# One of two lower parts of each u block subtracted by VectorE in place of TensorE

## The chip, the cores and the metric

The kernel runs on one core of one Trainium2 chip. The metric is the device time of one execution in microseconds (us), the median of the runs. A profiled execution gives, beside the time, the order of the instructions on each engine. Engines are named as in the profile: PE is TensorE (PEld its weight loads), DVE is VectorE, ACT is ScalarE, POOL is GpSimd, SP is SyncE, which here only starts DMAs.

## The reference

One step of an encoder layer for 1024 prompt tokens and 64 sample tokens: gated attention, convolution and memory branches, and then a retrieval of single-neuron experts (PEER). The change touches only the expert part, which computes, for tokens `xb` in blocks of 128:

```python
q = (xb @ w_q).reshape(B, PEER_HEADS, 2, PEER_DK // 2)
s1 = jnp.einsum('bhd,hkd->bhk', q[:, :, 0], keys1).astype(jnp.float32)
s2 = jnp.einsum('bhd,hkd->bhk', q[:, :, 1], keys2).astype(jnp.float32)
v1, i1 = lax.top_k(s1, PEER_TOPK)
v2, i2 = lax.top_k(s2, PEER_TOPK)
...
top, pos = lax.top_k(cand, PEER_TOPK)
idx = jnp.take_along_axis(cidx, pos, axis=-1)
g = jax.nn.softmax(top, axis=-1).astype(xb.dtype)
ue = u[idx]
ve = v[idx]
act = jax.nn.gelu(jnp.einsum('bd,bhkd->bhk', xb, ue), approximate=False)
return jnp.einsum('bhk,bhkd->bd', g * act, ve)
```

`u` and `v` are tables of 16384 rows of 1024 float32 numbers. Each token and each of 8 heads picks 16 rows of each.

## The kernel before

The front (projections), the attention and an opening stage for the first tile of tokens come first, up to about 1300 us. Then the function `experts` runs nine tiles of up to 128 tokens in steps, one step for one picked row per token. For the early tiles the step gathers a row of `u` for each token (GpSimd's indirect DMA, `u_row`), VectorE multiplies it with the token's normed row and sums (`dot`, line 3272), ScalarE applies gelu to four dots at a time (`gelu`, line 3088), and VectorE adds the gathered row of `v` times its weight (`vector_sum`, line 3295), eleven steps after the dot.

For the last four tiles (512 tokens, `TABLED`) no rows of `u` are gathered. TensorE computes instead the products of all 16384 rows of `u` with the 512 tokens, while the early tiles' steps go on. This is the table stage, steps 150 to 390 (`TABLE_STEPS`). The table of `u` is read in 128 blocks of 128 rows (`load_block`, a ring of three blocks). The products run in the reduced format fp32r, so each operand is split into an upper part (rounded to fp32r) and a lower part (what is left), and each product of two operands is three: upper by upper, upper by lower, lower by upper. For one block b:

- `turn_block` (line 2799): TensorE transposes the block's eight 128x128 squares into the PSUM tile `pH` (`open_h_T_ps`), four squares in each of two halves. A half is one PSUM bank of 128x512.
- `upper` (line 3017): ScalarE copies the half out of PSUM rounded to fp32r, into `B.uh`.
- `less_upper` (line 2805): TensorE adds to the same bank the product of minus identity with `B.uh`, so that the bank holds the lower part.
- `lower` (line 3021): ScalarE copies the bank into `B.ul`.
- `products` (line 2821): 8 x 3 products of 128x128 by 128x512 into the bank b % 2 of `pQS`.
- `stage_scores` (line 3028): ScalarE copies these scores to a buffer, which SyncE stores every fourth block.

The engines run their own lists of instructions in order. The lists are written by loops over the same step number n, and `units_at` spreads 257 table units over the 240 steps, for TensorE and for ScalarE alike: one unit opens the table, then each block has two. TensorE's unit 2b+1 holds `products(b, 0..3)` and the turn of half 0 of block b+1, its unit 2b+2 holds `products(b, 4..5)`, `less_upper` of half 0, the turn of half 1, `products(b, 6..7)` and `less_upper` of half 1. In 17 steps there are two units. In ScalarE's step n gelu comes before the table unit, exponentials of the routing (`exps`, line 2986) after it.

VectorE's step n holds the dot, the sum, and then the pieces of the routing (the two top-k, one hot rows and indices of the next heads, `route`), and three steps after a head's last piece its `gate` (line 3222), which waits for ScalarE's exponentials. VectorE has one piece of table work: `lower_h` (line 3323), the lower part of the 512 tokens' rows, at step 151.

After the table the scores are stored to memory and loaded again in another order (`load_scores`, line 2607), and picked from: TensorE, `pick_rows` (line 2878), VectorE, `picked` (line 3336), from step 398 on. The last tiles then sum rows of `v` on VectorE and on TensorE (`row_sum`, line 2904).

Of the kernel before, what the change touches and what calls it, by code (L numbers as in the profile page):

```python
# [13 lines left out]
F32 = mybir.dt.float32  # L14
# [7 lines left out]
P = 128  # L22
# [23 lines left out]
S0 = 1  # L46
# [2377 lines left out]
def experts(nc, io, scr, c, L, p, banks, done):  # L2424
# [29 lines left out]
    s_sck, s_const, s_pconst, s_hh, s_hl = (after() for _ in range(5))  # L2454
    s_uturn, s_uh, s_less, s_ul, s_block, s_stage = (after() for _ in range(6))
    s_keys, s_spread, s_skept, s_hot, s_pick, s_fpick, s_fold, s_tgelu, s_twt = (after() for _ in range(9))
    x_p = io["x_prompt"][0].rearrange("(t p) d -> t p d", p=P)[1:]
# [252 lines left out]
    def tensor(pe):  # L2710
# [81 lines left out]
        def turn_block(b, half):  # L2792
            pe.wait_ge(s_uin[b % TABLE_RING].sem, s_uin[b % TABLE_RING].start + 16 * (b // TABLE_RING + 1))
            if b:
                pe.wait_ge(s_ul.sem, s_ul.start + TURNS * (b - 1) + half + 1)
            else:
                pe.wait_ge(s_hT, S0 + NE + 1)
            for k in range(4):
                ins = pe.matmul(pH[:, half, k * P:(k + 1) * P], B.u[b % TABLE_RING][:, (4 * half + k) * P:(4 * half + k + 1) * P], c.ident[:],  # L2799
                                is_transpose=True, start=(k == 0), stop=False, skip_group_check=True)  # L2800
            ins.then_inc(s_uturn.sem, 1)

        def less_upper(b, half):
            pe.wait_ge(s_uh.sem, s_uh.start + TURNS * b + half + 1)
            pe.matmul(pH[:, half, :], B.minus[:], B.uh[b % 2][:, 4 * half:4 * half + 4, :].rearrange("p k i -> p (k i)"),  # L2805
                      start=False, stop=True, skip_group_check=True).then_inc(s_less.sem, 1)

        def products(b, ks):
            if ks[0] % 4 == 0:
                pe.wait_ge(s_ul.sem, s_ul.start + TURNS * b + ks[0] // 4 + 1)  # L2810
            if ks[0] == 0:
                if b >= 2:
# [12 lines left out]
        def table():  # L2825

            pe.wait_ge(s_const.sem, s_const.start + 1)
            for half in range(TURNS):
                turn_block(0, half)
                less_upper(0, half)  # L2830
            yield
            for b in range(NK):
# [5 lines left out]
                if b + 1 < NK:  # L2838
                    less_upper(b + 1, 0)
                    turn_block(b + 1, 1)  # L2840
                products(b, range(6, 8))
                if b + 1 < NK:
                    less_upper(b + 1, 1)
                yield

        def turn_keys(t):
            i = t - FIRST_TABLED
            pe.wait_ge(s_keys.sem, s_keys.start + NH * (i + 1))
            if i == 0:
                pe.wait_ge(s_const.sem, s_const.start + 2)  # L2850
                pe.wait_ge(s_ul.sem, s_ul.start + TURNS * NK)
            pe.wait_ge(s_skept.sem, s_skept.start + SPREADS * i)
# [79 lines left out]
    def scalar(act):  # L2932
# [85 lines left out]

        def lower(b, half):
            act.wait_ge(s_less.sem, s_less.start + TURNS * b + half + 1)  # L3020
            act.activation(B.ul[b % 2][:, 4 * half:4 * half + 4, :], pH[:, half, :].rearrange("p (k i) -> p k i", i=P), ACT.Copy).then_inc(s_ul.sem, 1)  # L3021

# [7 lines left out]
        def table():  # L3030
# [6 lines left out]
            act.activation(B.hh[:], B.h[:], ACT.Copy).then_inc(s_hh.sem, 1)  # L3037
            for half in range(TURNS):
                upper(0, half)
                lower(0, half)  # L3040
            yield
            for b in range(NK):
                if b + 1 < NK:
                    upper(b + 1, 0)
                yield
                if b + 1 < NK:
                    lower(b + 1, 0)
                    upper(b + 1, 1)
                    lower(b + 1, 1)
                stage_scores(b)  # L3050
                yield
# [69 lines left out]
    def vector(dve):  # L3121
# [198 lines left out]
        def lower_h():  # L3320

            dve.wait_ge(s_hh.sem, s_hh.start + 1)
            dve.tensor_tensor(B.hl[:], B.h[:], B.hh[:].bitcast(F32), ALU.subtract).then_inc(s_hl.sem, 1)

        def picked(t, g):
            i = PICKS * (t - FIRST_TABLED) + g
# [21 lines left out]
        tail = done.vector(dve, ahead)  # L3348
        front_units = front()
        for n in range(AHEAD_ROWS, STEPS + VECTOR_LAG):  # L3350
# [12 lines left out]
            for _ in units_at(FRONT_UNITS, FRONT_STEPS, n - 2):  # L3363
                next(front_units)
            if n == TABLE_STEPS[0] + 1:
                lower_h()
            for R, piece in ROUTES_AT.get(n, ()):
# [115 lines left out]
```

## Time and profile before

| | us |
|---|---|
| median of three runs | 3690.84 |
| lowest, highest | 3690.61, 3699.87 |
| span of the profiled execution | 3696.7 |
| its own time | 3699.87 |

The span goes from the first to the last instruction. The profiled execution's own time is the highest of the three, the only one that is not below the span; 3.2 us lie around the span. Busy times count an engine's instructions without waits. An idle time is put down to what released the engine at its end. Over the whole span the granted clock of TensorE is 0.950 in the mean.

### The profile page before, as it was taken

How to read it: one execution, taken by the hardware profiler on the slowest of the kernel's cores; microseconds unless marked ns; L12 is line 12 of the kernel's file. 1: busy time of each engine (PE TensorE's matmuls, PEld its weight loads, DVE VectorE, ACT ScalarE, POOL GpSimd, SP SyncE). 2: the span in 40 equal slices, each digit the busy share in tenths (PEclk: the TensorE clock that was granted, in tenths of full speed). 3: DMA queues.
4: the chain of work that ended last, by engine and by line, in shares of the span. 5: the costliest groups of instructions: out<-in, count | busy, mean ns of one | idle time of the engine just before them, and what ended most of it. 6: DMA issues, size and time to landing. Idle time of an engine off the chain costs nothing. (4 is left out here: it accounts for less than half of the span.)

```text
span 3696.7 us, 44443 instructions
## 1 busy us (share of the span) xinstructions
PE 3314.5 (90%) x13218; PEld 2187.7 (59%) x13218; DVE 2943.3 (80%) x6713; ACT 1413.4 (38%) x2912; POOL 2212.0 (60%) x1831
## 2 busy tenths in 40 slices
PE   8999899899999979988799999999968799988765
PEld 7787555544444446666688887888834355555321
DVE  5499764367887968999988898988889698987655
ACT  5235675222442322332444454445434333333200
POOL 6221144055565646777766675766656676777876
PEclk9999999999999989998899999999978899999989
DMA  6415564698999999999999999999999999999999
GB/s 213 127 40 147 137 179 174 207 359 315 350 376 384 340 382 349 375 383 374 408 400 403 379 405 406 388 401 388 395 403 357 361 373 391 390 387 360 333 366 344
DMA packets 443310, 1224.36 MB, mean 331 GB/s; under 512 B 65250, under 2 KB 153478, under 8 KB 442047
## 3 DMA queue, kind: packets, MB, share of 16 engines
q0 software_dynamic: 239616, 872.52, 61.7%
q1 hardware_dynamic: 177162, 313.45, 24.4%
q10 hardware_dynamic: 26293, 35.54, 2.8%
q8 instruction: 108, 1.77, 0.2%
q14 instruction: 131, 1.07, 0.1%
HBM read 1129.03 MB, written 92.31 MB: 330 GB/s over the span
## 5 line engine op out<-in xcount | busy, mean ns | idle before, releaser
L2679 POOL DMA_INDIRECT late_v_rows<-in_peer_v,late_kept_idx x573 | 605.3, 1056 | 195.2 <-issue 168.9
L2666 POOL DMA_INDIRECT late_u_rows<-in_peer_u,late_kept_idx x320 | 490.9, 1534 | 267.3 <-DVE late_dots L3272 187.9
L3272 DVE CUSTOM_DVE_ANT_0 late_u_rows<-late_u_rows,open_rows_ps 128x1024 f32<-128x1024 f32 x432 | 522.3, 1209 | 11.2 <-DMA late_u_rows<-in_peer_u,late_expert_idx 10.8
L3295 DVE SCALAR_TENSOR_TENSOR late_x<-late_v_rows,late_weights,late_x 128x1024 f32<-128x1024 f32 x368 | 471.2, 1280 | 0.0
L2821 PE MATMUL open_q_and_scores_ps<-table_h_T_upper,table_u_T_upper 128*128 128x512 f32 x1024 | 424.4, 415 | 0.0
L2821 PE MATMUL open_q_and_scores_ps<-table_h_T_lower,table_u_T_upper 128*128 128x512 f32 x1024 | 402.5, 393 | 0.0
L2821 PE MATMUL open_q_and_scores_ps<-table_h_T_upper,table_u_T_lower 128*128 128x512 f32 x1024 | 401.6, 392 | 0.0
L2679 POOL DMA_INDIRECT late_u_rows<-in_peer_v,late_kept_idx x259 | 293.8, 1134 | 93.5 <-issue 78.5
L1841 POOL DMA_INDIRECT open_u_rows<-in_peer_u,late_expert_idx x115 | 166.0, 1443 | 255.1 <-DVE late_dots L2281 125.9
L3295 DVE SCALAR_TENSOR_TENSOR late_x<-late_v_rows,table_weights,late_x 128x1024 f32<-128x1024 f32 x155 | 198.5, 1280 | 73.9 <-DMA late_v_rows<-in_peer_v,late_kept_idx 63.8
L2904 PE MATMUL open_sums_ps<-late_v_rows,table_diag 128*128 128x512 f32 (+1 forms) x328 | 184.1, 696 | 68.6 <-DMA late_v_rows<-in_peer_v,late_kept_idx 42.4
L3017 ACT ACTIVATE table_u_T_upper<-open_h_T_ps 128x512 fp32r<-128x512 f32 x256 | 152.4, 595 | 232.1 <-PE open_h_T_ps L2799 201.4
L3021 ACT ACTIVATE table_u_T_lower<-open_h_T_ps 128x512 fp32r<-128x512 f32 x256 | 152.9, 597 | 228.6 <-PE open_h_T_ps L2805 189.7
L3295 DVE SCALAR_TENSOR_TENSOR late_x<-late_u_rows,table_weights,late_x 128x1024 f32<-128x1024 f32 x138 | 176.9, 1282 | 65.7 <-DMA late_u_rows<-in_peer_v,late_kept_idx 59.5
L3065 ACT ACTIVATE table_apart<-open_h_T_ps,table_less_lane 128x512 bf16<-128x512 f32 x128 | 87.6, 684 | 362.1 <-PE open_h_T_ps L2862 241.9
L2821 PEld LDWEIGHTS open_q_and_scores_ps<-table_h_T_upper,table_u_T_lower 128*128 128x128 f32 x1024 | 192.9, 188 | 44.4
L2821 PEld LDWEIGHTS open_q_and_scores_ps<-table_h_T_lower,table_u_T_upper 128*128 128x128 f32 x1024 | 194.2, 190 | 32.6
L2821 PEld LDWEIGHTS open_q_and_scores_ps<-table_h_T_upper,table_u_T_upper 128*128 128x128 f32 x1024 | 193.9, 189 | 31.7
L497 POOL TENSOR_TENSOR front_w_lower<-front_w_raw,front_w_upper 128x512 fp32r<-128x512 f32 x62 | 94.7, 1546 | 193.5 <-ACT front_w_upper L721 192.4
L1177 POOL TENSOR_SCALAR attn_probs<-attn_probs,attn_row_scale 128x256 f32<-128x256 f32 (+2 forms) x68 | 93.1, 1374 | 171.7 <-DVE attn_row_scale L1290 171.7
L3336 DVE SCALAR_TENSOR_TENSOR table_masked<-table_row,table_first_keys,open_q_and_scores_ps 128x128 f32<-128x128 f32 x512 | 146.6, 342 | 51.7 <-DMA scr_mqT<-front_turned 28.1
L896 DVE SCALAR_TENSOR_TENSOR front_x_and_conv_y<-front_conv_input_T,front_conv_taps,front_x_and_conv_y 128x1118 f32<-128x1118 f32 x120 | 176.9, 1474 | 2.0
(471 smaller groups left out, 7803.0 us busy)
## 6 DMA issues: line engine op xcount, KB each, us to landing
table_u_block<-in_peer_u SPq DMA_DIRECT2D x128, 512.0 KB
scr_scores<-table_scores SPq DMA_DIRECT2D x32, 1024.0 KB
open_weight_columns<-in_w_in SPq DMA_DIRECT2D x64, 256.0 KB
table_first_scores<-scr_scores SPq DMA_DIRECT2D x4, 4096.0 KB
table_second_scores<-scr_scores SPq DMA_DIRECT2D x4, 4096.0 KB
front_w_raw<-in_w_in SPq DMA_DIRECT2D x48, 256.0 KB, 5.9
scr_m<-open_gated SPq DMA_DIRECT2D x42, 256.0 KB
late_v_rows<-in_peer_v,late_kept_idx POOLq DMA_INDIRECT x573
```

The costliest lines, as they stand in the source:

```text
L497: pool.tensor_tensor(wl[b][:, k, :], raw[:, k, :], wh[b][:, k, :].bitcast(F32), ALU.subtract).then_inc(s_wl, 1)
L896: ins = dve.scalar_tensor_tensor(yj, a[:, k:k + CONV_OUT], taps[:, j, k:k + 1], yj, ALU.mult, ALU.add)
L1841: pool.indirect_dma_start(O.u[b][:], None, io["peer_u"][0], bass.IndirectOffsetOnAxis(ap=rows_of(n), axis=0)).then_inc(s_u[b], 16)
L2666: pool.indirect_dma_start(u[k % U_RING][:], None, io["peer_u"][0], bass.IndirectOffsetOnAxis(ap=rows_of(n), axis=0)).then_inc(s_u[k % U_RI ...
L2679: pool.indirect_dma_start(slot[:], None, io["peer_v"][0], bass.IndirectOffsetOnAxis(ap=rows_of(m), axis=0)).then_inc(arrived, 16)
L2821: ins = pe.matmul(pQS[:, b % 2, 0:TABLE_COLS], us[b % 2][:, k, :], hs[:, k, :], start=(k == 0 and i == 0), stop=(k == KC - 1 and i == 2))
L2904: ins = pe.matmul(banks_of(t)[0:rows, h, :], diag[k % DIAGS][:, 0:rows], slot[:, h * BANK:(h + 1) * BANK], start=(m == first_of(t)), stop= ...
L3017: act.activation(B.uh[b % 2][:, 4 * half:4 * half + 4, :], pH[:, half, :].rearrange("p (k i) -> p k i", i=P), ACT.Copy).then_inc(s_uh.sem, 1)
L3021: act.activation(B.ul[b % 2][:, 4 * half:4 * half + 4, :], pH[:, half, :].rearrange("p (k i) -> p k i", i=P), ACT.Copy).then_inc(s_ul.sem, 1)
L3272: dve.tensor_tensor_reduce(u[k % U_RING][:], u[k % U_RING][:], h2_rows, 1.0, 0.0, ALU.mult, ALU.add, dots[:, n % COLS:n % COLS + 1]).then_ ...
L3295: dve.scalar_tensor_tensor(rows[:], slot[:], weight_of(m), rows[:], ALU.mult, ALU.add).then_inc(s_vsum, 1)
L3336: ins = dve.scalar_tensor_tensor(B.masked[:, q, :], B.row[:], B.first_keys[:, at:at + 1], pQS[:, i % 2, q * P:(q + 1) * P], ALU.is_equal, ...
```

## The change

The second half of each block (squares 4 to 7) is split in another way. TensorE turns it into its bank, ScalarE copies the upper part, and then VectorE reads the turned rows from PSUM, subtracts the upper part and writes the lower part to `B.ul` (`lower_half`), in one instruction of 128x512. TensorE's product with minus identity and ScalarE's second copy are left out for this half. The first half stays as it was. VectorE gets a list of table units on the same steps as the other engines: the unit that opens the table holds `lower_h` (one step earlier than before) and `lower_half(0)`, and the second unit of block b holds `lower_half(b + 1)`. It stands after the dot and the sum of its step and before the routing pieces. A new semaphore, `s_vl`, counts VectorE's halves; TensorE waits for it before `products(b, 4..)` and before it turns the next block's second half.

```diff
+    s_vl = p.sem("second_lower_halves")
...
         def turn_block(b, half):
             pe.wait_ge(s_uin[b % TABLE_RING].sem, s_uin[b % TABLE_RING].start + 16 * (b // TABLE_RING + 1))
-            if b:
-                pe.wait_ge(s_ul.sem, s_ul.start + TURNS * (b - 1) + half + 1)
+            if b and half:
+                pe.wait_ge(s_vl, S0 + b)
+            elif b:
+                pe.wait_ge(s_ul.sem, s_ul.start + b)
...
-        def less_upper(b, half):
-            pe.wait_ge(s_uh.sem, s_uh.start + TURNS * b + half + 1)
-            pe.matmul(pH[:, half, :], B.minus[:], B.uh[b % 2][:, 4 * half:4 * half + 4, :].rearrange("p k i -> p (k i)"),
+        def less_upper(b):
+            pe.wait_ge(s_uh.sem, s_uh.start + TURNS * b + 1)
+            pe.matmul(pH[:, 0, :], B.minus[:], B.uh[b % 2][:, 0:4, :].rearrange("p k i -> p (k i)"),
                       start=False, stop=True, skip_group_check=True).then_inc(s_less.sem, 1)
...
         def products(b, ks):
-            if ks[0] % 4 == 0:
-                pe.wait_ge(s_ul.sem, s_ul.start + TURNS * b + ks[0] // 4 + 1)
+            if ks[0] == 0:
+                pe.wait_ge(s_ul.sem, s_ul.start + b + 1)
+            elif ks[0] == 4:
+                pe.wait_ge(s_vl, S0 + b + 1)
...
@@ def table(): (TensorE)
                 products(b, range(4, 6))
                 if b + 1 < NK:
-                    less_upper(b + 1, 0)
+                    less_upper(b + 1)
                     turn_block(b + 1, 1)
                 products(b, range(6, 8))
-                if b + 1 < NK:
-                    less_upper(b + 1, 1)
...
@@ def table(): (ScalarE)
                 if b + 1 < NK:
-                    lower(b + 1, 0)
+                    lower(b + 1)
                     upper(b + 1, 1)
-                    lower(b + 1, 1)
                 stage_scores(b)
...
+        def lower_half(b):
+            dve.wait_ge(s_uh.sem, s_uh.start + TURNS * b + 2)
+            if b >= 2:
+                dve.wait_ge(s_block.sem, s_block.start + b - 1)
+            dve.tensor_tensor(B.ul[b % 2][:, 4:8, :], pH[:, 1, :].rearrange("p (k i) -> p k i", i=P), B.uh[b % 2][:, 4:8, :].bitcast(F32), ALU.subtract).then_inc(s_vl, 1)
+
+        def table():
+
+            lower_h()
+            lower_half(0)
+            yield
+            for b in range(NK):
+                yield
+                if b + 1 < NK:
+                    lower_half(b + 1)
+                yield
...
-            if n == TABLE_STEPS[0] + 1:
-                lower_h()
+            for _ in units_at(TABLE_UNITS, TABLE_STEPS, n):
+                next(table_units)
```

## Rows read from the trace of the kernel before

**Rows 1.** The page, part 1: busy us (share of the span) and instructions by engine.

```profile
PE 3314.5 (90%) x13218; PEld 2187.7 (59%) x13218; DVE 2943.3 (80%) x6713; ACT 1413.4 (38%) x2912; POOL 2212.0 (60%) x1831
```

**Rows 2.** Busy by stretch: us; PE, PEld, DVE, ACT, POOL; clock; DMA share; GB/s.

```profile
1784.00:2694.00 910.00, 890.33 (x4352) 727.54 (x4352) 794.63 (x1798) 443.38 (x810) 605.74 (x487) 0.99 1.02 397
2260.00:2300.00 40.00, 35.68 (x165) 28.87 (x164) 36.09 (x87) 16.27 (x30) 27.56 (x24) 0.91 1.03 411
```

**Rows 3.** Waits, 1784 to 2694 us: waiter, releaser, us in all, times, longest.

```profile
ACT table_u_T_upper L3017 <- PE open_h_T_ps L2799: 201.4, 111, 6.9
...
POOL late_u_rows L2666 <- DVE late_dots L3272: 172.5, 106, 11.3
DVE late_exp_scale L3222 <- ACT late_exps L2986: 104.0, 23, 9.9
...
PE open_h_T_ps L2805 <- ACT table_u_T_upper L3017: 12.9, 9, 7.7
...
DVE late_exp_scale L3222 <- issue: 1.3, 1, 1.3
```

**Rows 4.** Instruction groups, same stretch: count, busy us, mean ns, idle before.

```profile
L3295 DVE SCALAR_TENSOR_TENSOR late_x<-late_v_rows,late_weights,late_x 128x1024 f32<-128x1024 f32 x242 | 309.9, 1281 | 0.0
L3272 DVE CUSTOM_DVE_ANT_0 late_u_rows<-late_u_rows,open_rows_ps 128x1024 f32<-128x1024 f32 x242 | 292.5, 1209 | 0.4
...
L3021 ACT ACTIVATE table_u_T_lower<-open_h_T_ps 128x512 fp32r<-128x512 f32 x256 | 152.9, 597 | 228.6 <-PE open_h_T_ps L2805 189.7 <-issue 35.9 <-DVE late_side_idx L3150 2.0
```

**Rows 5.** Score evictions (ns, first and last start); one block in order of time.

```profile
L3028 ACT ACTIVATE table_scores<-open_q_and_scores_ps x128: 589/592/598, 1805.4 to 2693.9; 128x512 f32<-128x512 f32 x128
...
2203.56 0.59 ACT L3028 ACTIVATE table_scores<-open_q_and_scores_ps 128x512 f32<-128x512 f32 x1
...
2207.46 0.40 PE L2805 MATMUL open_h_T_ps<-table_u_T_upper,table_minus_identity 128*128 128x512 f32 x1
2207.69 0.60 PE L2799 MATMUL open_h_T_ps<-identity,table_u_block 128*128 128x128 f32 x4
...
2210.45 0.59 ACT L3028 ACTIVATE table_scores<-open_q_and_scores_ps 128x512 f32<-128x512 f32 x1
```

**Rows 6.** Front subtraction (group); two neighbours in VectorE's queue, order of time.

```profile
L834 DVE TENSOR_TENSOR front_turned_lower<-front_turned_ps,front_turned 128x512 f32<-128x512 f32 x6 | 4.1, 683 | 0.0
...
2282.20 0.69 DVE L3181 TENSOR_TENSOR late_one_hot<-late_pos_split_f,late_iota 128x512 f32<-128x512 f32 x1
2282.81 1.22 DVE L3272 CUSTOM_DVE_ANT_0 late_u_rows<-late_u_rows,open_rows_ps 128x1024 f32<-128x1024 f32 x1
```

**Rows 7.** Order of time at the start of the table stage.

```profile
1782.75 1.28 DVE L3295 SCALAR_TENSOR_TENSOR late_x<-late_v_rows,late_weights,late_x 128x1024 f32<-128x1024 f32 x1
...
1784.55 3.60 ACT L3037 ACTIVATE table_h_T_upper<-table_h_T 128x4096 fp32r<-128x4096 f32 x1
...
1788.18 4.43 DVE L3323 TENSOR_TENSOR table_h_T_lower<-table_h_T,table_h_T_upper 128x4096 fp32r<-128x4096 f32 x1 [0.77 <-ACT table_h_T_upper L3037]
...
1795.03 0.60 ACT L3017 ACTIVATE table_u_T_upper<-open_h_T_ps 128x512 fp32r<-128x512 f32 x1 [0.25 <-PE open_h_T_ps L2799]
```

**Rows 8.** VectorE, order of time: step 388, first picks, a late row.

```profile
2680.32 1.20 DVE L3272 CUSTOM_DVE_ANT_0 late_u_rows<-late_u_rows,open_rows_ps 128x1024 f32<-128x1024 f32 x1
...
2726.36 0.35 DVE L3336 SCALAR_TENSOR_TENSOR table_masked<-table_row,table_first_keys,open_q_and_scores_ps 128x128 f32<-128x128 f32 x1 [7.97 <-PE open_q_and_scores_ps L2878]
...
2740.55 1.28 DVE L3295 SCALAR_TENSOR_TENSOR late_tile_sum<-late_v_rows,late_weights,late_tile_sum 128x1024 f32<-128x1024 f32 x1 [5.34 <-issue]
```

**Rows 9.** ScalarE, order of time: a table load and its gelu.

```profile
1599.86 1.28 ACT L3088 ACT_TABLE_LOAD   x1
1604.93 0.20 ACT L3088 ACTIVATE late_gelu<-late_dots 128x4 f32<-128x4 f32 x1 [3.79 <-DVE late_dots L3272]
```

**Rows 10.** Order of time around 2270 and 2280 us.

```profile
2269.88 0.51 PE L2805 MATMUL open_h_T_ps<-table_u_T_upper,table_minus_identity 128*128 128x512 f32 x1 [0.24 <-ACT table_u_T_upper L3017]
...
2280.43 0.60 ACT L3017 ACTIVATE table_u_T_upper<-open_h_T_ps 128x512 fp32r<-128x512 f32 x1 [6.86 <-PE open_h_T_ps L2799]
```

More of the change, by code:

```diff
@@ L2799, in turn_block @@
                 ins = pe.matmul(pH[:, half, k * P:(k + 1) * P], B.u[b % TABLE_RING][:, (4 * half + k) * P:(4 * half + k + 1) * P], c.ident[:],
-                                is_transpose=True, start=(k == 0), stop=False, skip_group_check=True)
+                                is_transpose=True, start=(k == 0), stop=(half == 1 and k == 3), skip_group_check=True)
             ins.then_inc(s_uturn.sem, 1)
-        def less_upper(b, half):
-            pe.wait_ge(s_uh.sem, s_uh.start + TURNS * b + half + 1)
-            pe.matmul(pH[:, half, :], B.minus[:], B.uh[b % 2][:, 4 * half:4 * half + 4, :].rearrange("p k i -> p (k i)"),
+        def less_upper(b):
+            pe.wait_ge(s_uh.sem, s_uh.start + TURNS * b + 1)
+            pe.matmul(pH[:, 0, :], B.minus[:], B.uh[b % 2][:, 0:4, :].rearrange("p k i -> p (k i)"),
                       start=False, stop=True, skip_group_check=True).then_inc(s_less.sem, 1)
         def products(b, ks):
-            if ks[0] % 4 == 0:
-                pe.wait_ge(s_ul.sem, s_ul.start + TURNS * b + ks[0] // 4 + 1)
+            if ks[0] == 0:
+                pe.wait_ge(s_ul.sem, s_ul.start + b + 1)
+            elif ks[0] == 4:
+                pe.wait_ge(s_vl, S0 + b + 1)
             if ks[0] == 0:
@@ L2827, in table @@
             pe.wait_ge(s_const.sem, s_const.start + 1)
-            for half in range(TURNS):
-                turn_block(0, half)
-                less_upper(0, half)
+            turn_block(0, 0)
+            less_upper(0)
+            turn_block(0, 1)
             yield
@@ L2850, in turn_keys @@
                 pe.wait_ge(s_const.sem, s_const.start + 2)
-                pe.wait_ge(s_ul.sem, s_ul.start + TURNS * NK)
+                pe.wait_ge(s_ul.sem, s_ul.start + NK)
+                pe.wait_ge(s_vl, S0 + NK)
             pe.wait_ge(s_skept.sem, s_skept.start + SPREADS * i)
@@ L3017, in upper, with lower @@
             act.activation(B.uh[b % 2][:, 4 * half:4 * half + 4, :], pH[:, half, :].rearrange("p (k i) -> p k i", i=P), ACT.Copy).then_inc(s_uh.sem, 1)
-        def lower(b, half):
-            act.wait_ge(s_less.sem, s_less.start + TURNS * b + half + 1)
-            act.activation(B.ul[b % 2][:, 4 * half:4 * half + 4, :], pH[:, half, :].rearrange("p (k i) -> p k i", i=P), ACT.Copy).then_inc(s_ul.sem, 1)
+        def lower(b):
+            act.wait_ge(s_less.sem, s_less.start + b + 1)
+            act.activation(B.ul[b % 2][:, 0:4, :], pH[:, 0, :].rearrange("p (k i) -> p k i", i=P), ACT.Copy).then_inc(s_ul.sem, 1)
         def stage_scores(b):
@@ L3037, in table @@
             act.activation(B.hh[:], B.h[:], ACT.Copy).then_inc(s_hh.sem, 1)
-            for half in range(TURNS):
-                upper(0, half)
-                lower(0, half)
+            upper(0, 0)
+            lower(0)
+            upper(0, 1)
             yield
@@ L3348, in vector @@
         tail = done.vector(dve, ahead)
-        front_units = front()
+        front_units, table_units = front(), table()
         for n in range(AHEAD_ROWS, STEPS + VECTOR_LAG):
```

## The prediction

> **What bounds the kernel now.** I first read the table of engines for the whole span [rows 1]: no engine is at its limit everywhere, so the stage that the change touches is read by itself. The busy time by stretch over the table stage (1784 to 2694 us) shows TensorE busy for 890.3 of 910 us, VectorE for 794.6, ScalarE for 443.4, at a granted clock of 0.99 [rows 2]. The waits of the same stretch say who waits for whom [rows 3]: TensorE's longest row of waits is 12.9 us, while VectorE waits 104.0 us in 23 pieces for `late_exps` of ScalarE. ScalarE does those exponentials behind its table work, and the table work waits for TensorE (201.4 us before `upper`, 189.7 before `lower`, [rows 3, 4]). So VectorE runs ahead, is held at each head's gate, and TensorE sets the pace. GpSimd waits for VectorE's dots (172.5 us), and neither dots nor sums show VectorE waiting for a gathered row (0.4 and 0.0 us) [rows 4]: the gathers are not what ends last here, though DMA moves 397 GB/s.
>
> TensorE's pace is in the order of time [rows 5]: the 128 score evictions start from 1805.4 to 2693.9 us, 7.00 us apart in the mean, and two undisturbed neighbours are 2210.45 - 2203.56 = 6.89 us apart. The product with minus identity holds TensorE for 0.23 us, from its start to the next (2207.46 to 2207.69), and I take the same for each of the 24 products of that width.
>
> **What goes.** One 128x512 product per block leaves TensorE: 128 x 0.23 = 29.4 us, all on the path as long as TensorE sets the pace. Its block becomes 6.89 - 0.23 = 6.66 us. One eviction of 0.597 us per block leaves ScalarE (128 x 0.597 = 76 us, [rows 4]): ScalarE is busy less than half the stage, so this is worth nothing by itself; it only lets the remaining evictions and exponentials start sooner.
>
> **What comes.** 128 subtractions of 128x512 on VectorE, one input in PSUM, output in fp32r. The table stage has none, but the front does the same subtraction (turned PSUM tile less its upper part): 683 ns [rows 6]. In a full queue the next instruction starts sooner: a 0.69 us operation at 2282.20 is followed by one at 2282.81 [rows 6], so one costs 0.61 us net; bounds 0.61 and 0.69. I take 0.61, since VectorE's queue is full there: 128 x 0.61 = 78.1 us (88 at the upper bound). A rule that speaks against the change: the Trainium skill, "VectorE: DVE Perf Modes", section "The DRAIN you can't avoid", says that the next operation doesn't start until the pipe of the last has emptied. If that charged the whole 0.683 us the sum would come out 9 us later; the starts 0.61 us apart in the row contradict it here, so the row is used.
>
> **Who bounds after it.** VectorE waits 104.0 + 1.3 + 0.77 = 106.1 us of the stage [rows 3, 7]; these waits exist because it is ahead, and they go when it isn't. Work of VectorE outside those waits: 910 - 106.1 = 803.9 us, plus 78.1 = 882. TensorE by itself: 128 x 6.66 = 852 plus its stalls. So VectorE becomes the bound, and it is tied to TensorE block by block: `lower_half(b+1)` waits for ScalarE's upper copy, which waits for TensorE's turn in the same step, while TensorE's products 4 to 7 wait for `lower_half`. Behind the waiting subtraction stand VectorE's routing pieces, the next dot and the next sum; for the dots wait GpSimd's gathers and ScalarE's gelu.
>
> **The start.** In the old order VectorE subtracts `h_T` at step 151 with 0.77 us of wait. Now its first unit stands in step 150: its sum there ends at 1784.03, the upper copy of h at 1788.15, so it waits 4.1 us; the subtraction ends at 1792.6 [rows 7]. The second upper copy of block 0 ends at 1795.6 [rows 7], so `lower_half(0)` waits another 3.1 us. 7.2 us of waits come (the old 0.77 is in the 106.1).
>
> **The end of the stage.** Before, VectorE reaches its first picked rows with 7.97 us of idle time before 2726.36, so its last work ended at 2718.4 [rows 8]. That wait is for a chain from the last product (2693.9) through the score eviction, store and load to the first pick: 32.4 us. New arrival of VectorE: 2718.4 - 106.1 + 7.2 + 78.1 = 2697.6. New end of the chain: the dot of step 388 was at 2680.32 [rows 8]; it comes at 2680.3 - 106.1 + 7.2 + 77.5 = 2658.9; dot, sum and the last `lower_half` take 2.3 + 0.1 + 0.6, twelve products 2.8, then 32.4: 2697.1. The two meet. Against 2726.4 both are 28.8 us early. After that every engine has the same work, and the rings of rows tie them together, so I let the shift pass to the end. One gathered row comes 5.34 us late at 2740.55 [rows 8]; that may move by as much either way.
>
> **What coupling gives back.** (a) Gelu stands in ScalarE's queue every fourth step ahead of the copies, and waits for the dot of that step, which so far was long done. With VectorE last it is not. In about 30 of 60 cases it stands before the copy that `lower_half` waits for: gelu 0.20 and two copies 0.5 + 0.6, with a hand-off, 1.5 us, beside VectorE's sum of 1.28: 0.2 us each, 6 us. The table load is not in it: the one at 1599.86 ran before gelu's 3.79 us wait [rows 9]. (b) 257 units lie in 240 steps, so 17 steps hold two. There two `lower_half` are one step of VectorE's work apart (803.9 / 240 = 3.35 us). From one `lower_half` TensorE needs six products (1.4), `less_upper` (0.23) and a turn (0.60), ScalarE 0.60 and a hand-off, to make the next one possible: 3.0 us, and up to 4.7 where gelu stands between. I take 0.3 us each, 5 us. (c) The u blocks behind the store and load of a tile's sums come late once: `upper` at 2280.43 stands after 6.86 us of idle time [rows 10]. Now VectorE, which had been in front, feels it, less TensorE's lead of some 3 us: 4 us. (d) 127 hand-offs where the queue no longer overlaps fully: 3 us. Sum 18 us; ends 2 us (all hidden) and 41 us (0.3 us per block more than I take: the nearest row is the 0.24 us of idle that TensorE shows between an upper copy's end and its product, 2269.88 [rows 10]).
>
> So -28.8 + 18 = -10.8 us. The profiled execution has a span of 3696.7 us and 3.2 us around it, 3699.87 in all, and would take 3689.1. It lies 9.0 us above the median, 3690.84; taken from that the time is 3680.
>
> **Rivals.**
> *TensorE remains the bound (0.15).* If the subtractions hide in the 106.1 us of waits, 127 x 0.23 = 29 us are won: 3662. For it: 106.1 is more than 78.1. Against it: the waits come from being ahead, and the start and the coupling take 25 us of the rest.
> *The loop closes badly, slower (0.20).* The place is ScalarE's queue: gelu(n) waits for dot(n), the copy for `lower_half(b+1)` waits behind gelu, and VectorE stands at it. Priced at 0.2 us for 30 blocks above; if each costs 1.0 us, and the odd steps (where gelu holds TensorE's `less_upper`) 0.5 us, it is 45 us for 6: -10.8 + 39 = +28, 3719; at 0.6 us each and nothing for the odd steps, 18 for 6, it is +1. It decides from about 0.6 us per coincidence. For it: the lead that kept ScalarE from waiting (VectorE's waits reach 9.9 us, [rows 3]) vanishes. Against it: in a block of two steps VectorE needs 2 x 3.35 + 0.61 = 7.3 us from one `lower_half` to the next, and the copy is there after 3.0 to 4.7.
> *The losses equal the gain (0.10).* No mechanism but the sum of (a) to (d) near 29 us: 3691.
> *TensorE's clock (0.10).* With VectorE as the bound TensorE idles 0.3 us a block. After the long stall the granted clock over 2260 to 2300 was 0.91 against 0.99 in the stage [rows 2], which puts part of it at the lower level, 1.2 GHz. If such spells, worth some 3.5 us each, come ten times, TensorE is late by 35 us; its slack against VectorE is 882 - 852 = 30 us over the whole stage, little of it where a spell falls, and I let it take a third: +23 - 10.8 = +12, 3703. By the Trainium skill's page "TensorE: Matmul & The Clock Gate", Part 1, the throttled rate is the default and activity releases it; by that rule idle time spread thinly costs nothing, and the stage's 0.99 agrees as far as it goes.
> *The change doesn't do what it says:* the products' order and every wait's count follow the removed signals; I see no way for it.
>
> **Numbers.** The forecast's own case has 0.45; its own range is 3670 to 3691. Of it 0.27 lies beyond 0.3% (11 us, about what this measurement can tell from no change) and 0.18 within. Faster: 0.27 + 0.15 = 0.42. Same: 0.18 + 0.10 = 0.28. Slower: 0.20 + 0.10 = 0.30. The range reaches down to the first rival, 3662, and up to 3703, which leaves out the far part of the second.
>
> **What would show it.** `less_upper` x128 instead of 256; VectorE's subtraction near 0.68 us; waits for `late_exps` in the stage below 15 us in place of 104; new idle time of TensorE before products (4..5) until VectorE, of some 0.3 us per block; VectorE busy over 96% of the stage; the last score eviction near 2683 in place of 2693.9, and the first picked rows near 2715. Wrong, if VectorE still waits over 60 us in the stage, at `lower_half` above all, or if TensorE's clock shows new spells at the lower level.

## The result and the profile after

The changed kernel takes 3708.7 us in the median of 20 runs, the kernel before 3698.47 in 20 runs beside it. The ratio is 1.0028, with a 95% interval of 1.0019 to 1.0037: about 10 us slower. A second batch of runs gave 1.0038 (1.0022 to 1.0053). The forecast was 10.8 us faster, 3680 us, with a range up to 3703. (It was counted from 3690.84, the median of three runs; the differences here are from the 20.) The profiled execution took 3722.61 us, 14 above its median, so the argument below goes by stretches of it and not by its end.

The waits of the changed kernel, 1784 to 2720 us (waiter, what released it, us in all, times, longest), answer to [rows 3]:

```profile
ACT table_u_T_upper L3021 <- PE open_h_T_ps L2802: 216.7, 95, 5.3
POOL late_u_rows L2667 <- DVE late_dots L3275: 190.6, 178, 12.7
ACT late_gelu L3091 <- DVE late_dots L3275: 132.8, 52, 8.8
ACT table_u_T_lower L3025 <- PE open_h_T_ps L2808: 80.7, 88, 1.0
...
DVE table_u_T_lower L3332 <- ACT table_u_T_upper L3021: 28.4, 22, 4.0
...
PE open_q_and_scores_ps L2826 <- ACT table_u_T_lower L3025: 22.3, 22, 2.2
...
PE open_h_T_ps L2808 <- ACT table_u_T_upper L3021: 17.7, 15, 7.7
...
PE open_q_and_scores_ps L2826 <- DVE table_u_T_lower L3332: 0.6, 2, 0.3
```

VectorE's 104 us of waits for the exponentials are gone altogether: VectorE no longer runs ahead, as forecast. Three rows are new. VectorE waits 28.4 us for the upper copies. ScalarE's gelus, which had no row in this stretch, wait 132.8 us for VectorE's dots. And TensorE waits 22.3 us at the first product of a block for `lower`, ScalarE's copy of the first half. Its wait at `less_upper` (line 2805 before, 2808 now) grew from 12.9 us to 17.7, of which 7.7 lie at the start in both kernels. For VectorE's half, where some 0.3 us per block had been forecast, it waits 0.6 us in all.

The new subtraction, in the group rows (us busy, mean ns, idle before), and the same stretch from the dot of step 150 to the dot of step 388, first the kernel before, then the changed one, then its second trace. Columns as in [rows 2].

```profile
L3332 DVE TENSOR_TENSOR table_u_T_lower<-open_h_T_ps,table_u_T_upper 128x512 fp32r<-128x512 f32 x128 | 87.8, 686 | 31.6 <-ACT table_u_T_upper L3021 28.4 <-issue 2.1
```

```profile
1781.60:2680.30 898.70, 876.73 (x4291) 716.94 (x4292) 783.46 (x1772) 439.12 (x801) 596.83 (x480) 0.99 1.02 397
```

```profile
1784.70:2691.90 907.20, 859.84 (x4196) 696.73 (x4197) 862.25 (x1897) 378.60 (x682) 613.00 (x480) 0.99 1.02 395
```

```profile
1785.50:2693.40 907.90, 861.92 (x4196) 698.73 (x4197) 862.41 (x1899) 378.39 (x682) 613.12 (x480) 0.98 1.02 394
```

The stretch is 8.5 us longer (907.2 against 898.7), and the second trace repeats it within 0.7 us. VectorE's busy time rose by 862.25 - 783.46 = 78.8 us, to 95.0% of the stretch; TensorE's is nearly the same (859.84 us), so the two engines set the pace between them. From the dot of step 388 to that of step 447 the two kernels take the same, 202.1 us before and 201.7 after. So the loss up to step 447 lies in the table stage, and it is about as large as the loss of the whole. Behind step 447 the time differs from one batch to the next whatever the kernel (the changed kernel took 827 us in the first trace and 787 in the second), and nothing is argued from it.

Adding up VectorE's idle times in that stretch by their length gives this account (worked out from the trace's single instructions):

| VectorE, steps 150 to 388, us | before | changed |
|---|---|---|
| busy | 783.5 | 862.2 |
| waits over 0.5 us | 106.1 | 32.2 |
| shorter gaps | 9.2 | 12.7 |
| sum | 898.7 | 907.2 |

Of the 32.2 us, 7.2 lie at the start, 4.0 at the late u block at step 279, and 21.0 in fourteen waits at the subtraction, of which twelve (17.6 us; at steps 178, 193, 206, 221, 249, 262, 292, 305, ...) stand within one step of a step that holds two table units. The other two (3.4 us, at steps 195 and 223) stand behind table loads of ScalarE, which are shown further down.

### The profile page after: what moved, and what is told of

Read it like the earlier page. It is cut to its first block and busy times, and to the rows that moved or that the text cites. A ratio compares the mean times of both kernels' runs of the same rounds, so it can differ in the third digit from the quotient of the medians.

```text
span 3720.8 us, 44315 instructions
## 1 busy us (share of the span) xinstructions
PE 3288.5 (88%) x13090; PEld 2162.4 (58%) x13090; DVE 3021.8 (81%) x6841; ACT 1348.2 (36%) x2784; POOL 2239.0 (60%) x1831
## 5 line engine op out<-in xcount | busy, mean ns | idle before, releaser
L2667 POOL DMA_INDIRECT late_u_rows<-in_peer_u,late_kept_idx x320 | 509.1, 1591 | 261.1 <-DVE late_dots L3275 209.3
L2826 PE MATMUL open_q_and_scores_ps<-table_h_T_upper,table_u_T_upper 128*128 128x512 f32 x1024 | 426.7, 417 | 23.0 <-ACT table_u_T_lower L3025 22.3
L2680 POOL DMA_INDIRECT late_u_rows<-in_peer_v,late_kept_idx x259 | 301.7, 1165 | 94.1 <-issue 73.4
L2908 PE MATMUL open_sums_ps<-late_u_rows,table_diag 128*128 128x512 f32 x248 | 133.7, 678 | 51.0 <-DMA late_u_rows<-in_peer_v,late_kept_idx 47.8
```

Source lines behind the costliest of these rows:

```text
L2667: pool.indirect_dma_start(u[k % U_RING][:], None, io["peer_u"][0], bass.IndirectOffsetOnAxis(ap=rows_of(n), axis=0)).then_inc(s_u[k % U_RI ...
L2680: pool.indirect_dma_start(slot[:], None, io["peer_v"][0], bass.IndirectOffsetOnAxis(ap=rows_of(m), axis=0)).then_inc(arrived, 16)
L2908: ins = pe.matmul(banks_of(t)[0:rows, h, :], diag[k % DIAGS][:, 0:rows], slot[:, h * BANK:(h + 1) * BANK], start=(m == first_of(t)), stop= ...
```

## Experiments

The stage figures below are VectorE's times from the dot of step 150 to that of step 388, as above.

### The load without the waits

```diff
 (on the kernel before)
+        def unread(b):
+            ...
+            dve.wait_ge(s_un, S0 + b)
+            dve.tensor_tensor(tile_sum[:, 0:BANK], pRows[:, 1, :], keysT[:, 0:4, :].rearrange("p s k -> p (s k)"), ALU.subtract).then_inc(s_un, 1)
...
+            for _ in units_at(TABLE_UNITS, TABLE_STEPS, n):
+                next(table_units)
```

> The kernel before, with VectorE's 128 subtractions of 128x512 added at the places of the change, but into a tile that nobody reads and with no other engine waiting; TensorE and ScalarE keep all their work. Theory A (the load of 78 us fits into VectorE's 106 us of waits, what hurts is the order in which the three engines now wait for each other): the time of before within 0.15% (ratio 0.999 to 1.002), TensorE's pace still 6.87 us a block, VectorE's waits for the exponentials down from 104 to some 20 to 35 us. Rival B (the load alone does it, VectorE is full and GpSimd's gathers and the rest come late): 8 us or more slower, ratio 1.002 to 1.004, as the changed kernel.

Ratio 1.0010 (0.9999 to 1.0022), 3701.72 us against 3698.67. The stage took 896.6 us, 2.1 less than before. VectorE's waits in the stage:

```profile
DVE late_exp_scale L3223 <- ACT late_exps L2987: 25.8, 14, 5.1
DVE late_exp_scale L3223 <- issue: 1.9, 1, 1.9
```

```profile
1779.20:2675.80 896.60, 877.00 (x4299) 717.80 (x4300) 859.58 (x1897) 440.67 (x804) 616.35 (x480) 0.99 1.02 399
```

VectorE is as busy as in the changed kernel (859.6 us) and the stage isn't longer. The waits for the exponentials fell from 104.0 to 25.8, by the 78 us added. As long as TensorE keeps its old work and sets the pace, the load alone does nothing to the stage; Theory A holds there. The whole time's interval doesn't exclude a loss of up to 8 us, so that part is only bounded.

### The waits without the load

```diff
 (on the changed kernel)
-            dve.tensor_tensor(B.ul[b % 2][:, 4:8, :], pH[:, 1, :]...
+            if b < 2:
+                dve.tensor_tensor(B.ul[b % 2][:, 4:8, :], pH[:, 1, :]...
+            else:
+                dve.tensor_tensor(B.ul[b % 2][:, 4, 0:4], pH[:, 1, 0:4], B.uh[b % 2][:, 4, 0:4].bitcast(F32), ALU.subtract).then_inc(s_vl, 1)
```

> The changed kernel, but from block 2 on VectorE subtracts 4 columns in place of 512, so that all waits stay and most of the load goes (the lower parts of the second halves are then not computed). Theory A (waits between the engines): about 0.5 us per block go from VectorE, 60 us of 78; as VectorE's work was the bound together with the waits, the stage falls to TensorE's pace of about 6.65 us per block or a little above: 20 to 27 us faster than before, ratio 0.9930 to 0.9950, if the waits by themselves cost little without the load; if it stays within 5 us of before the waits alone hold it. Rival B (load): the full 25 to 29 us of TensorE's saving appear, 0.9925 or less.

Ratio 0.9979 (0.9962 to 0.9995); the stage took 880.9 us, 26.3 less than the changed kernel's and 17.8 less than before, with 62 us less for VectorE to do. Both expectations (0.9950 or less) were too good. But neither the load alone nor the waits alone makes the stage longer than before: it takes the two together, at this place in the step. Waits for rows of `v` came up that the changed kernel doesn't have:

```profile
DVE table_u_T_lower L3335 <- ACT table_u_T_upper L3021: 37.1, 22, 6.0
DVE late_x L3298 <- DMA late_v_rows<-in_peer_v,late_kept_idx: 9.5, 14, 2.2
DVE late_x L3298 <- issue: 8.4, 10, 1.8
```

At this pace the gathered rows of `v` come late, 18 us in 24 waits. This comes back in the last experiments.

### The subtraction one unit later

```diff
             lower_half(0)
             for b in range(NK):
+                if b:
+                    lower_half(b)
                 yield
-                if b + 1 < NK:
-                    lower_half(b + 1)
                 yield
```

> The changed kernel with each block's subtraction one table unit later in VectorE's list, that is, one step. Nothing is added or left out. Theory A: VectorE's 25 us of waits at the subtraction (14 of them at the steps with two units) fall below 8 us, since TensorE and ScalarE have a step more to deliver, and the stage shortens by 15 to 20 us against the changed kernel: ratio to before 0.9970 to 0.9995. Rival C (TensorE then waits as long for VectorE as VectorE did for ScalarE, since the half that it needs comes a step later): no better than the changed kernel, 1.002 to 1.004.

Ratio 0.9969 (0.9954 to 0.9985), stage 884.7 us: 22.5 us less than the changed kernel with the very same instructions. VectorE's waits over 0.5 us are 13.1 in place of 32.2, and TensorE's wait for VectorE's half, the price that Rival C named, is 14.3 us in 25 waits, where TensorE has slack. Rival C falls, and the gain is a little above Theory A's range (15 to 20 us, 0.9970). Of the waits at the subtraction 9.2 us are left, where under 8 were expected. The rows, up to 2700 us, which is behind the stage (the waits of 8.8 and 15.4 us lie there):

```profile
ACT late_gelu L3091 <- DVE late_dots L3275: 30.2, 20, 8.8
PE open_sums_ps L2908 <- ACT table_diag L3086: 15.4, 1, 15.4
PE open_q_and_scores_ps L2826 <- DVE table_u_T_lower L3332: 14.3, 25, 1.6
...
DVE table_u_T_lower L3332 <- ACT table_u_T_upper L3021: 9.2, 7, 3.1
```

### Every second block

On the changed kernel, with `by_dve(b)` for `b % 2 == 1`; the other blocks' second halves keep `less_upper` and ScalarE's `lower`.

```diff
-            if b and half:
-                pe.wait_ge(s_vl, S0 + b)
+            if b and half and by_dve(b - 1):
+                pe.wait_ge(s_vl, S0 + dve_halves(b))
...
                 products(b, range(6, 8))
+                if b + 1 < NK and not by_dve(b + 1):
+                    less_upper(b + 1, 1)
```

> The changed kernel, but only every second block's second half is subtracted by VectorE; the others keep TensorE's product and ScalarE's copy. VectorE gets 39 us in place of 78, TensorE is spared 15 us in place of 29. Theory A: VectorE has some 40 us left over, so its waits cost nothing and TensorE remains the bound: 8 to 14 us faster than before, ratio 0.996 to 0.998. Rival C (each wait of the new kind costs by itself): half of the changed kernel's loss, ratio 1.0005 to 1.0015.

Ratio 0.9984 (0.9969 to 0.9998), just outside Theory A's 0.996 to 0.998. The stage took 898.0 us, as before, so Theory A is wrong there: VectorE waits 59.3 us at the subtraction, and the 15 us that TensorE is spared don't show. With slack in VectorE its place in the step still ties the engines.

### The changed kernel again, and gelu behind the unit

Where does a wait at a doubled step come from? ScalarE, TensorE and VectorE of the changed kernel in order of time, around the wait at step 348:

```profile
2540.42 0.20 ACT L3091 ACTIVATE late_gelu<-late_dots 128x4 f32<-128x4 f32 x1 [2.42 <-DVE late_dots L3275]
2540.53 0.58 ACT L3025 ACTIVATE table_u_T_lower<-open_h_T_ps 128x512 fp32r<-128x512 f32 x1
...
2541.16 0.50 PE L2826 MATMUL open_q_and_scores_ps<-table_h_T_upper,table_u_T_upper 128*128 128x512 f32 x1 [0.38 <-ACT table_u_T_lower L3025]
...
2541.63 0.69 DVE L3332 TENSOR_TENSOR table_u_T_lower<-open_h_T_ps,table_u_T_upper 128x512 fp32r<-128x512 f32 x1
...
2546.07 0.60 PE L2802 MATMUL open_h_T_ps<-identity,table_u_block 128*128 128x128 f32 x4
...
2546.77 0.59 ACT L3021 ACTIVATE table_u_T_upper<-open_h_T_ps 128x512 fp32r<-128x512 f32 x1
...
2547.39 0.69 DVE L3332 TENSOR_TENSOR table_u_T_lower<-open_h_T_ps,table_u_T_upper 128x512 fp32r<-128x512 f32 x1 [1.41 <-ACT table_u_T_upper L3021]
```

Gelu waits 2.42 us for VectorE's dot. Behind it in ScalarE's queue stands `lower`, the copy of the first half, and TensorE can't begin the next block's first product without it (2541.16). So when VectorE does its subtraction at 2541.63, TensorE has only begun the twelve products that it could have had behind it. It still has to do those, a turn, six more, `less_upper` and a turn before ScalarE can copy, and VectorE, one step later, waits 1.41 us.

The way is not the same at all twelve doubled steps. Ahead of each, TensorE has waited for a copy that stood behind a waiting gelu: one step before at four of them, for `lower` (0.4 to 2.2 us); two steps before at five, at `less_upper` for the upper copy (0.5 to 1.3 us); three steps before at the last three (178, 206, 262), for `lower` again (0.6 to 1.8 us). What they share is that TensorE comes late to the `less_upper` of the next block: 2.1 to 4.4 us behind the end of VectorE's last subtraction (from the single instructions). From there to the end of the upper copy it is 1.52 us every time.

At steps 195 and 223 ScalarE's queue holds a table load between the exponentials and gelu, ahead of both copies. ScalarE and VectorE around step 223:

```profile
2068.77 1.28 ACT L3091 ACT_TABLE_LOAD   x1
2070.07 0.20 ACT L3091 ACTIVATE late_gelu<-late_dots 128x4 f32<-128x4 f32 x1
2070.18 0.58 ACT L3025 ACTIVATE table_u_T_lower<-open_h_T_ps 128x512 fp32r<-128x512 f32 x1
...
2071.28 0.69 DVE L3332 TENSOR_TENSOR table_u_T_lower<-open_h_T_ps,table_u_T_upper 128x512 fp32r<-128x512 f32 x1 [2.16 <-ACT table_u_T_upper L3021]
```

The next run moves gelu, with its table loads, behind both copies:

```diff
 (ScalarE's step n, on the changed kernel)
-            if n % GROUP == GROUP - 1 and n < STEPS and dotted(n):
+            if n % GROUP == GROUP - 1 and n < STEPS and dotted(n) and not TABLE_STEPS[0] < n < TABLE_STEPS[1]:
                 gelu(n // GROUP)
...
             for _ in units_at(TABLE_UNITS, TABLE_STEPS, n):
                 next(table_units)
+            if n % GROUP == GROUP - 1 and TABLE_STEPS[0] < n < TABLE_STEPS[1]:
+                gelu(n // GROUP)
```

> The changed kernel once more, beside the others of this batch, for a second trace of it. Both theories: ratio to before 1.002 to 1.004; VectorE from the dot of step 150 to that of step 388 in 903 to 911 us (907.2 in the first trace), 12 or more waits of over 0.5 us at the subtraction, nearly all in or next to a step with two table units.

> The changed kernel with ScalarE's gelu of a step placed behind the table unit of that step in place of ahead of it, in the table stage. Theory D (the waits at the steps with two units come from gelu: it waits for VectorE's dot, the lower copy of half 0 queues behind it, TensorE waits for that copy before its first product and so is late when two units fall into one step): VectorE's waits at the subtraction fall from 28 us to 8 to 15, steps 150 to 388 take 886 to 895 us in place of 907, ratio to before 0.9965 to 1.000. Rival E (what is missing at those steps is the time that TensorE and ScalarE need for two units, 3.0 us at the least, against one step of VectorE, gelu or not): the waits stay above 20 us, ratio 1.0015 or more.

The changed kernel again: 1.0038 (1.0022 to 1.0053), stage 907.9 us, sixteen waits at the subtraction, 28.6 us. With gelu behind the unit: 0.9995 (0.9980 to 1.0010), stage 884.5 us, the waits at the subtraction 9.0 us in five. Rival E falls: the time that two units need isn't what was missing. At nine of the same twelve blocks the upper copy now ends 3.06 to 3.25 us behind the last subtraction, where it was 3.6 to 5.9 us before the move. The rows up to 2700 us, again with two waits behind the stage (8.8 and 18.6 us):

```profile
ACT late_gelu L3091 <- DVE late_dots L3277: 28.9, 16, 8.8
PE open_sums_ps L2908 <- ACT table_diag L3086: 18.6, 1, 18.6
PE open_q_and_scores_ps L2826 <- DVE table_u_T_lower L3334: 14.0, 25, 1.3
DVE table_u_T_lower L3334 <- ACT table_u_T_upper L3021: 9.4, 7, 3.7
```

Inside the stage gelu's waits for the dots fall from 119 us in the first trace of the changed kernel (129 in the second) to 15, and TensorE waits for VectorE's half in place of ScalarE's copies, which means that it is nearly always as far ahead as it can be. The run shows that gelu's place is the cause; it doesn't part the ways by which gelu held the others, since gelu stands behind both copies now.

The gain over the changed kernel is 23 us in the stage and some 16 us (1.0038 to 0.9995) in the time. 3.5 us of it are given back between steps 388 and 447 (205.2 us for 201.7); the rest is not explained. Against the kernel before, no gain in the time is shown (the interval holds 1), though the stage is 14 us shorter. One unit later, with as long a stage, has 0.9969, so gelu behind the unit may cost something outside the stage.

### Both together

One unit later and gelu behind the unit.

> Both: the subtraction one unit later and gelu behind the table unit. Theory D: with one unit later nearly all of the waits were gone already (13 us left, 7 of them at the start of the stage), so there is little to add: steps 150 to 388 in 880 to 886 us (884.7 with one unit later alone), ratio within 0.001 of that one's 0.9969. Rival E: the same, since both say that slack is all that counts; a time clearly over it would say that gelu behind the unit does harm elsewhere.

Ratio 0.9983 (0.9969 to 0.9997), stage 886.0 us. Nothing is added, as expected: each edit alone gives the slack. The ratio lies 0.0014 above that of one unit later alone, outside the 0.001 stated, but the two were run in different batches and the intervals overlap.

### Every second block, one unit later

> VectorE subtracts only every second block's second half, and one unit later. Theory A: TensorE is the bound with 15 us saved, VectorE has slack: steps 150 to 388 in 884 to 890 us, 10 to 14 us under before, ratio 0.9965 to 0.9980; no better than one unit later with all blocks, whose bound is VectorE at 885. Rival C (each wait costs by itself, and fewer of them are better): faster than one unit later with all blocks, below 0.9960.

Ratio 0.9961 (0.9947 to 0.9975), stage 882.8 us, 2 us shorter than with all blocks. This version beats both kernels, by 14 us the kernel before. Theory A's ranges (884 to 890 us, 0.9965 or more) were too slow by a little, and Rival C's (below 0.9960) isn't reached. Against one unit later with all blocks (0.9969, another batch) no difference is shown.

### What is late next

Four more on that version: the store of a tile's sums split from the load behind it, the second load of scores later, both, and both with three of four blocks.

```diff
             if b in AFTER_BLOCK:
-                t = AFTER_BLOCK.index(b)
-                store_y(t)
+                store_y(AFTER_BLOCK.index(b))
+            if b - 4 in AFTER_BLOCK:
+                t = AFTER_BLOCK.index(b - 4)
                 load_x2(t + 2)
                 load_h2(t + 2)
```

> Built on the version with every second block and one unit later (every_second_later, ratio 0.9961). Its one edit: the load of the next tile's sums and rows is issued four u blocks after the store that it waits for, so that SyncE's queue doesn't hold back the loads of u blocks for 16 us. Theory: the long block near 2275 us (TensorE 6 to 7 us late, VectorE some 4 us in the changed kernel) goes; steps 150 to 388 take 876 to 879 us in place of 882.8; ratio 0.9940 to 0.9958. Rival (the u blocks' loads are late for want of bandwidth at that place, not for the wait): the stage stays at 881 or more.

Ratio 0.9979 (0.9966 to 0.9993), stage 881.3 us. VectorE's long wait for the late u block at step 280 (7.5 us) is 0.7 us now, so the wait did come from SyncE's queue. But the stage is only 1.5 us shorter, where 4 to 7 were expected; it stays at the 881 or more that the rival named, and the whole time shows no gain. The theory is right about the wait and wrong about its worth. What took its place:

```profile
DVE table_u_T_lower L3355 <- ACT table_u_T_upper L3040: 23.0, 18, 3.4
...
DVE late_x L3321 <- DMA late_v_rows<-in_peer_v,late_kept_idx: 10.1, 16, 1.5
DVE late_x L3321 <- issue: 6.4, 5, 2.0
```

Rows of `v` come late, which in the version before this edit showed no row. The stretch moves 406 GB/s:

```profile
1791.10:2672.40 881.30, 862.24 (x4248) 707.32 (x4249) 824.51 (x1833) 411.80 (x743) 600.26 (x480) 0.99 1.03 406
```

```diff
-        load_scores(FIRST_TABLED)
+        load_scores(FIRST_TABLED, (0,))
         store_y(SHORT - 1)
+        load_scores(FIRST_TABLED, (1,))
...
+                elif k == 0:
+                    sp.wait_ge(s_pick.sem, s_pick.start + 2)
```

> Built on every_second_later. Its one edit: the second of the two loads of 4 MB of scores starts only when two groups have been picked. Theory F (the gathered row of step 401 or so is late since it stands behind 8 MB of scores in the DMA engines): VectorE's waits at the sums between steps 398 and 404 fall from 9.3 us to under 5 us, the dot of step 447 comes 3 to 7 us earlier behind that of 388 than the 204.7 us there. Rival G (a row or a pick is late anyway, since the same bytes have to be moved): the sum of the waits there stays above 13 us of 15.7 and 447 comes 204 us or more behind 388.

Ratio 0.9960 (0.9936 to 0.9985), stage 882.6 us. From step 388 to 447 the time is 202.2 us, 2.5 less than 204.7, and the waits there are 6.4 us at the pick and 6.8 at a row of step 405, 13.2 in place of 15.7. Neither expectation fits whole: the waits at the sums of steps 398 to 404 are gone, as Theory F had it, but less than 3 us are gained and the sum of the waits stays above 13, as Rival G had it. The late row moves from step 401 to 405 and stays.

> Both edits on every_second_later. If they are independent: the sum of the two gains, 6 to 12 us under every_second_later, ratio 0.993 to 0.9950; steps 150 to 388 as in the first, 388 to 447 as in the second. If one of them only moves the wait elsewhere: no faster than the better of the two.

Ratio 0.9978 (0.9964 to 0.9992): no faster than the better of the two, as the second expectation has it. What is left of each is not followed further.

> Both edits, and VectorE subtracts the second halves of three of four blocks in place of one of two: 20 us more for VectorE, 7 us less for TensorE. TensorE's sum is then 128 x 6.70 = 857 us with some 10 us of stalls, VectorE's 804 + 59 = 863 with 7 at the start: near balance. Theory: steps 150 to 388 in 868 to 878 us, 2 to 8 us under the version with one of two. Rival H (near balance each engine's unevenness is felt by the other, and rows come late at that pace): no faster than one of two, or slower.

Ratio 0.9978 (0.9967 to 0.9989), stage 884.7 us. VectorE waits 15.4 us for rows of `v` and 8.4 for the copies. Rival H holds: no faster than one of two.

## Why the prediction was wrong

**What bounds, what goes, what comes.** These steps held up to small differences. TensorE's block went from 6.87 to 6.61 us where nothing held it; the subtraction took 686 ns where 683 was read from the front, and raised VectorE's busy time by 78.8 us where 128 x 0.61 = 78.1 was forecast. The waits for the exponentials vanished. The overlap of queued operations in the row is what counted: 128 x 0.686 = 87.8 without it. The sentence that the prediction took from the Trainium skill ("VectorE: DVE Perf Modes", the section "The DRAIN you can't avoid") would give the larger figure, and the trace does not agree with it. The same section goes on to say that a next operation which isn't held starts earlier, and the starts 0.61 us apart, for 0.69 us of duration [rows 6], fit that.

**The start** held: 4.2 and 3.1 us.

**What coupling gives back** failed. It was put at 18 us: (a) 6, (b) 5, (c) 4, (d) 3. Measured are (c) 4.0, (d) 3.5, and 21.0 us in fourteen waits for (a) and (b) together: 17.6 at the doubled steps, where (b) had 5 us, and 3.4 at the two table loads. (a), a small wait in each of 30 ordinary blocks, hardly came in that form. The step that failed is (b), with 17 x 0.3 us for what took 1.5 us in each of twelve: "From one `lower_half` TensorE needs six products (1.4), `less_upper` (0.23) and a turn (0.60)" takes TensorE to be as far ahead as it may be at each doubled step. It wasn't: from one `lower_half` to the next upper copy's end it took 3.6 to 5.9 us, and with gelu moved the 3.0 us came out (3.06). Gelu holds ScalarE's `lower` and so TensorE's first product (22.3 us), and, as the second rival had it, the upper copy and so `less_upper` (10 us besides the start, 5 us before the change). In (a) and (b) I had gelu and the two copies behind it only as time until the next `lower_half`, never as what holds TensorE's first product a block earlier. Gelu behind the unit and the subtraction one unit later, with the same work, each took some 23 us off the stage.

"The table load is not in it" failed as well. The load of [rows 9] ran while ScalarE would have waited for the dot anyway; at steps 195 and 223 ScalarE had no such wait, the load stood ahead of the copies, and VectorE waited 1.26 and 2.16 us.

**The end of the stage** failed too. "Against 2726.4 both are 28.8 us early" shortens the way from step 388 to the end by 7.4 us beyond the stage's 21.4, by taking away VectorE's wait at the picks. That wait did vanish, and another took its place: a gathered row two sums ahead of the one that had been 5.34 us late [rows 8] is late by 11.59 us, ahead of the picks, and the old one by 0.84. VectorE, changed kernel, in order of time:

```profile
2721.69 1.27 DVE L3298 SCALAR_TENSOR_TENSOR late_tile_sum<-late_v_rows,late_weights,late_tile_sum 128x1024 f32<-128x1024 f32 x1
...
2738.84 1.28 DVE L3298 SCALAR_TENSOR_TENSOR late_tile_sum<-late_v_rows,late_weights,late_tile_sum 128x1024 f32<-128x1024 f32 x1 [11.59 <-issue]
2742.59 0.35 DVE L3356 SCALAR_TENSOR_TENSOR table_masked<-table_row,table_first_keys,open_q_and_scores_ps 128x128 f32<-128x128 f32 x1
```

The waits between steps 388 and 447 were 13.3 us before and are 12.4 now, and they are 13 to 16 in one unit later and in every second block, one unit later, with and without the second load later. I had seen a late row and treated it as noise of 5 us. Whether these rows and the scores are late for the same transfers is not shown: the run with the second load later moved the late row and didn't remove it.

The terms against the forecast: coupling 28.5 us in place of 18 (10.5), the end of the stage 0.4 us in place of 7.4 (7.0), together 17.5 of the 21 us between -10.8 and +10.2. VectorE's load adds 1.3 us (78.8 for the 77.5 up to step 388); the rest is within the intervals.

**What would show it.** Of the signs, `less_upper` x128, the subtraction's 0.68 us and the vanished waits for the exponentials came. VectorE was busy 95.0% of the stage in place of over 96; TensorE's small waits for VectorE's half didn't come; the last score eviction was at 2698.7 us in place of about 2683, and the first picked rows at 2742.6 in place of about 2715. The two signs that would have called it wrong (60 us of VectorE's waits, new clock spells) didn't come either: the forecast failed between them.

**The rivals.** The direction came from the one that was given 0.20: the place was ScalarE's queue with gelu in it, as named. The way was only in part the named one (VectorE at the copy in every other block), so that its price came near (21 us for about 11, where it wanted about 0.6 us in each of 30 blocks) is partly luck: it was 1.5 us in each of fourteen. The point from which it decides was set too high since 7.4 us that weren't there stood in the sum. TensorE's clock was no factor: 0.99 in the stage in both first traces, and 0.98 in the second of the changed kernel, whose stage is as long. That VectorE can be the bound and the stage still shorten by 14 us is shown by one unit later, close to the -10.8 forecast.

## What to carry to other kernels

Moving work to an engine that waits a lot also takes away the lead that its waits stand for; list every in-order queue that waits for that engine, and everything behind each such wait. Place the moved work so that there is a step of slack on both sides: here the same instructions, one step later in the list, went from 10 us slower than before to 11 us faster. Before a stage is shortened by a few per cent, look at what lies just under it, since several engines can be within 2% of each other (here 862.2 and 859.8 us busy).

## What the runs showed of the hardware

In the table stage the DMA engines may be a third bound just under TensorE and VectorE. Nine versions with different work or order for TensorE and VectorE ended between 880.9 and 886.0 us at 403 to 406 GB/s, where the kernel before moved 397 in 898.7. The higher rate is only the same bytes in less time and proves no limit by itself. What speaks for one is that in the four shortest or most evenly loaded of them (the waits without the load, and the three with the split store) gathered rows of `v` come late, by 16 to 18 us in all. That the rows are late for want of bandwidth is read from this, and wasn't tested by itself, as no run moved fewer bytes.

A table load of ScalarE takes 1.28 us. It cost nothing where ScalarE was going to wait for VectorE's dot anyway (3.79 us of wait behind the load, [rows 9]), and stood in full ahead of the copies where it wasn't (2068.77, above).
